# Expert layers by pairs: two experts of 64 token slots each on the two column halves of the matmul array, in float32 on unsplit weights

## The reference

```
lg = xt @ w_rg + b_rg                      # 4 groups; grp = argmax
le = (xt @ w_re + b_re) of that group      # 8 experts in a group; top 2 of softmax
gate = top_p / sum(top_p) * p_grp
for each expert e of 32:
    y_e = (silu(x_e @ w_eg[e]) * (x_e @ w_eu[e])) @ w_ed[e]     # 1024 -> 512 -> 1024
out[token] = sum over its two experts of gate * y_e[token]
```

## Time and profile before

| | us |
|---|---|
| median of three runs | 2326.18 |
| span of the profiled execution, first to last instruction | 2329.0 |
| PE busy in it | 2235.9 |
| `mix_out`, `route`, experts (from the timeline) | 382.9 to 428.1, to 454.4, to 999.3 |

### The profile page before, as it was taken

One profiled execution on the slowest core, in us unless ns is written; L12 is line 12 of the kernel. 1 busy time (PEld: TensorE's weight loads), 2 busy tenths in 40 slices (PEclk: granted clock), 3 DMA queues, 4 the chain that ended last, 5 costly groups with the idle time before them and its releaser, 6 DMA issues. The chain is left out here.

```text
span 2329.0 us, 30346 instructions
## 1 busy us (share of the span) xinstructions
PE 2235.9 (96%) x11961; PEld 1898.9 (82%) x11961; DVE 1801.5 (77%) x2133; ACT 1161.0 (50%) x1215; POOL 138.8 (6%) x237
## 2 busy tenths in 40 slices
PE   7999989999999999999999999999998999999997
PEld 7888768788888888888788887888987888887886
DVE  6887687688989889866888777887796887776545
ACT  4443244577677776744444364333653333464332
POOL 2000100000000000000111001110001111000000
PEclk9999998999999999999999999999999999999999
DMA  8854553499999999954799536994633998445652
GB/s 300 272 138 148 177 172 100 154 375 375 368 372 375 363 376 363 364 165 154 228 373 350 165 114 210 375 349 169 208 127 112 333 357 289 141 129 166 196 181 72
DMA packets 346769, 567.83 MB, mean 244 GB/s; under 512 B 69248, under 2 KB 182400, under 8 KB 346624
## 3 DMA queue, kind: packets, MB, share of 16 engines
q1 hardware_dynamic: 325632, 490.31, 62.0%
q0 software_dynamic: 20992, 75.54, 8.7%
HBM read 564.71 MB, written 1.05 MB: 243 GB/s over the span
## 5 line engine op out<-in xcount | busy, mean ns | idle before, releaser
L321 PE MATMUL ps<-st_hi,sb_h_hi 128*128 128x512 f32 (+1 forms) x728 | 272.1, 374 | 11.7 <-DVE sb_h_lo L1187 4.6
L323 PE MATMUL ps<-st_hi,sb_h_lo 128*128 128x512 f32 (+1 forms) x728 | 265.0, 364 | 0.0
L322 PE MATMUL ps<-st_lo,sb_h_hi 128*128 128x512 f32 (+1 forms) x728 | 264.8, 364 | 0.0
L293 DVE TENSOR_TENSOR es_lo<-es_raw,es_hi 128x2048 fp32r<-128x2048 f32 x87 | 196.9, 2284 | 19.3 <-ACT es_hi L283 18.9
L321 PE MATMUL ps<-ring_hi,sb_h_hi 128*128 128x512 f32 (+1 forms) x504 | 191.2, 379 | 4.2 <-DVE sb_h_lo L832 2.1
L323 PE MATMUL ps<-ring_hi,sb_h_lo 128*128 128x512 f32 (+1 forms) x504 | 188.5, 374 | 0.0
L322 PE MATMUL ps<-ring_lo,sb_h_hi 128*128 128x512 f32 (+1 forms) x504 | 188.2, 373 | 0.0
L293 DVE TENSOR_TENSOR ring_lo<-ring_raw,ring_hi 128x2048 fp32r<-128x2048 f32 (+4 forms) x86 | 155.2, 1806 | 39.8 <-ACT ring_hi L283 39.7
L293 DVE TENSOR_TENSOR st_lo<-ring_raw,st_hi 128x2048 fp32r<-128x2048 f32 (+1 forms) x66 | 148.9, 2255 | 42.8 <-ACT st_hi L283 42.8
L283 ACT CAST es_hi<-es_raw 128x2048 fp32r<-128x2048 f32 x87 | 164.6, 1914 | 23.9 <-DMA es_raw<-in_w_expert_up_dram 17.9
L293 DVE TENSOR_TENSOR st_lo<-st_raw,st_hi 128x2048 fp32r<-128x2048 f32 x64 | 146.3, 2288 | 30.9 <-ACT st_hi L283 30.8
(11 more groups left out here) (798 smaller groups left out, 5383.6 us busy)
## 6 DMA issues: line engine op xcount, KB each, us to landing
t_aw<-in_ada_w_dram POOLq DMA_DIRECT2D x144, 512.0 KB, 6.6
st_raw<-in_ffn_w_in_dram SPq DMA_DIRECT2D x90, 512.0 KB, 5.8
ring_raw<-in_ffn_w_in_dram SPq DMA_DIRECT2D x86, 512.0 KB, 6.0
es_raw<-in_w_expert_gate_dram SPq DMA_DIRECT2D x40, 1024.0 KB, 8.2
es_raw<-in_w_expert_down_dram SPq DMA_DIRECT2D x39, 1024.0 KB, 7.4
es_raw<-in_w_expert_up_dram SPq DMA_DIRECT2D x37, 1024.0 KB, 7.4
ring_raw<-in_w_expert_up_dram SPq DMA_DIRECT2D x27, 1024.0 KB, 7.2
ring_raw<-in_w_expert_down_dram SPq DMA_DIRECT2D x25, 1024.0 KB, 7.2
```

Source lines behind the costliest of these rows:

```text
L293: dve.tensor_tensor(p.at(self.lo[m % self.held]), p.at(self.raw[n % self.slots]), p.at(self.hi[m % self.held]).bitcast(F32), ALU.subtract) ...
L321: pe.matmul(out, a_hi, b_hi, start=start, stop=False, skip_group_check=True)
L322: pe.matmul(out, a_hi, b_lo, start=False, stop=False, skip_group_check=True)
L323: return pe.matmul(out, a_lo, b_hi, start=False, stop=stop, skip_group_check=True)
```

## The change

Experts are taken by pairs, 16 of them. Each expert has 64 slots of its own (before: 128 slots for a group of eight experts). The slots of the two experts of a pair are the two halves of the array's columns: one matmul has 64 stationary columns and writes partitions 0 to 63, the next writes 64 to 127, and each streams the weights of its own expert. They are float32 matmuls on the raw pieces, with no split on ACT and DVE and no `hi` and `lo` (all pieces are `plain`). The ring has 15 raw slots. The result of a pair is split (`y_hi`, `y_lo`) and scattered to all tokens after each pair; slots of two pairs (four experts, a unit) are gathered from the tokens two pairs ahead (`draw`), between the matmuls of the running pair. Weights lie in slots with the row index split as `(p k)`, so that a partition takes 8 KB in one stretch (before 2 KB or 4 KB stretches). `route` ranks tokens by expert instead of by group, on 64 and 80 columns. The pass for overflow now counts experts with over 64 tokens. The first three pieces go out at the start of `mix_out`, ahead of its last four, and `route` sends the next twelve. The core of the diff:

```diff
 def expert_plan(A):
-    deep = lambda w: w.rearrange("(k p) n -> p k n", p=P)
-    for e in range(NG * NE + 1):
-        if e < NG * NE:
-            pieces += [Piece(deep(w[e, a * P:(a + 4) * P, :]), 4, BANK) for w in (wg, wu) for a in (0, 4)]
-        if e:
-            pieces += [Piece(deep(wd[e - 1, u * HB:(u + 1) * HB, :]), 2, 1024) for u in range(2)]
+    deep = lambda w: w.rearrange("(p k) n -> p k n", p=P)
+    for p in range(NP + 1):
+        if p < NP:
+            pieces += [Piece(deep(w[e])[:, a:a + 4, :], 4, BANK, True)
+                       for w in (wg, wu) for a in (0, 4) for e in (2 * p, 2 * p + 1)]
+        if p:
+            pieces += [Piece(deep(wd[e])[:, f:f + 2, :], 2, 1024, True) for f in (0, 2) for e in (2 * p - 2, 2 * p - 1)]
...
+def gather(pe, M, out, perm, c):
+    for i in (2 * c, 2 * c + 1):
+        for w in range(2):
+            for t in range(2):
+                last = pe.matmul(out[:, i % 2 * 256:(i % 2 + 1) * 256], (M.h_hi, M.h_lo)[w][:, t, i:1024:8],
+                                 perm[:, t].rearrange("p x s -> p (x s)"), start=w == t == 0, stop=w == t == 1,
+                                 skip_group_check=True)
...
 (route, SP)
-            S.send(sp, S.slots + 1)
+            S.send(sp, lent + 2)
...
 (experts, PE)
-            def half(e, bank, a):
-                w = S.take(pe)
+            def half(p, bank, a):
+                w = [S.take(pe), S.take(pe)]
                 for kt in range(a, a + 4):
-                    last = product(pe, ps[:, bank, :], M.hg_hi[:, e // NE, kt, :], M.hg_lo[:, e // NE, kt, :],
-                                   w[0][:, kt - a, :], w[1][:, kt - a, :], kt == 0, kt == 7)
-                last.then_inc(S.used, 1)
+                    for h in range(2):
+                        at = (p % 2 * 2 + h) * SL
+                        last = pe.matmul(ps[h * SL:(h + 1) * SL, bank, :], M.hg[p // 2 % 2][:, kt, at:at + SL],
+                                         w[h][:, kt - a, :], start=kt == 0, stop=kt == 7, skip_group_check=True)
+                        if kt == a + 3:
+                            last.then_inc(S.used, 1)
...
+            def down(p, u):
+                w = [S.take(pe), S.take(pe)]
...
+                for f in (2 * u, 2 * u + 1):
+                    for c in range(2):
+                        for h in range(2):
+                            part = slice(h * SL, (h + 1) * SL)
+                            last = pe.matmul(ps[part, sum_bank(p) + c, :], hidT[:, f, part],
+                                             w[h][:, f - 2 * u, c * BANK:(c + 1) * BANK], start=f == 0, stop=f == NF - 1,
+                                             skip_group_check=True)
...
+            for p in range(NP):
+                v = unit_of(p)
+                if p:
+                    pe.wait_ge(silued, p)
+                half(p, 0, 0)
+                if p:
+                    turn(p - 1)
+                if v:
+                    draw(v, 3 * (p % 2))
+                half(p, 0, 4)
+                if p >= 2:
+                    scatter(p - 2, 0)
...
+                half(p, 1, 0)
+                if v:
+                    draw(v, 3 * (p % 2) + 1)
+                if p >= 2:
+                    scatter(p - 2, 1)
+                half(p, 1, 4)
+                if p:
+                    down(p - 1, 0)
+                if v:
+                    draw(v, 3 * (p % 2) + 2)
+                if p:
+                    down(p - 1, 1)
...
 (mix_out, SP)
+            k.experts.send(sp, 3)
             S.send(sp, len(S.pieces))
...
-        k.stream = Stream(nc, "es", expert_plan(A), UNIT, k.shared, (None, None, 0, 1, None), (0, None, None, None)).place(own)
+            k.experts = Stream(nc, "es", expert_plan(A), UNIT, k.shared, (None,) * 13 + (0, 1), ()).place(k.far, "right", 3)
```

More of the change, by code:

```diff
@@ L1382 @@
 HB = 256
+NP, SL = NG * NE // 2, 64
 def expert_plan(A):
@@ L1420, in route @@
[L1420 to L1423, removed]
+        wr, br = k.wr, k.br
+        lt, rest, hit, one, two = (sb(n, [P, NT * R, NE]) for n in ("lt", "rest", "hit", "one", "two"))
+        asg, both = sb("asg", [P, NT, NG, NE]), sb("both", [P, NT, NG, NE])
+        m1, m2, b1 = (sb(n, [P, NT * R]) for n in ("m1", "m2", "b1"))
+        desc, ss, zg = sb("desc", [P, NE]), sb("ss", [P, NT]), sb("zg", [P, NT])
@@ L1488, in _ @@
             pe.wait_ge(q["placed"], 1)
[L1489 to L1509, removed]
+            for c in range(4):
+                gather(pe, M, ps[:, c, :], M.perm[0], c).then_inc(q["gathered"], 1)
+            turn_places(k, pe, ps[:, 4, :], M.perm[0]).then_inc(q["gathered"], 1)
             pe.wait_ge(q["weighted"], 1)
[L1511 to L1514, removed]
+            slot_gates(pe, M, ps[:, 5, :], M.perm[0], 0).then_inc(q["gathered"], 1)
         @block.scalar
@@ L1612, in _ @@
[L1612 to L1622 removed]
+            after(dve.tensor_tensor(both[:], one_e, wide(w1[:]), ALU.mult))
@@ L1847, in program @@
-            copy(n * U + 1, 1)
-        guarded(act, found, program)
-    def vector_pass(dve, found):
-        def take(kind, b, u):
-            dve.wait_ge(high[kind], b + 1)
-            dve.tensor_tensor(lo[kind], raw[u][kind], hi[kind].bitcast(F32), ALU.subtract
-                              ).then_inc(split[kind], 1)
-        def expert(i, n, m, j, final=False):
-            for u in range(U):
-                b = n * U + u
-                more = not (final and u == 1)
-                if more:
-                    take(G, b + 1, 1 - u)
@@ L1862, in expert @@
                 dve.wait_ge(filled[UP], b + 1)
                 dve.wait_ge(silued, b + 1)
[L1865 to L1876 removed]
+                at = M.late_gate[:, m, i:i + 1] if isinstance(i, int) else M.late_gate[:, m, bass.ds(i, 1)]
@@ L1945, in _ @@
             for n in range(2):
-                sp.wait_ge(S.split, S.order[len(S.pieces) - 5 + n] + 1)
+                slot = S.slots - 2 + n
+                final = max(m for m in range(len(S.pieces)) if m % S.slots == slot)
+                sp.wait_ge(S.used, final + 1)
                 N2.send(sp, n + 1)
@@ L2015, in _ @@
+            turn(NP - 1)
+            for c in range(2):
+                last = pe.matmul(ps[:, c, :], k.ones[:], k.gates[:, 1, c * BANK:(c + 1) * BANK], start=True, stop=True)
+            last.then_inc(row_summed, 1)
+            found = first_of(pe)
+            scatter(NP - 2, 0)
+            down(NP - 1, 0)
+            scatter(NP - 2, 1)
+            down(NP - 1, 1)
             late_tensor(pe, found)
-            pe.wait_ge(added, 4 * (NG - 1))
+            pe.wait_ge(added, 4 * (NP - 1))
```

725 lines of the change are left out of this document (325 added, 400 removed).

## The result

The changed kernel takes 2239.23 us (median of four runs, 2238.60 to 2240.18) against 2326.26 us, a ratio of 0.9623 (95% interval 0.9609 to 0.9637). The gain is 87 us. The prediction was 60 us, with 31 to 88 as the likeliest case's own range: sign and mechanism are right, the size is at the far end of that range, one microsecond inside it (the range on record went from 2232 to 2345 us). The profiled execution took 2239.4 us and has a span of 2237.6 us; the span is the shorter one by 1.8 us, as in the other runs of both kernels. So the profiled execution of the kernel before, with its span of 2329.0, was some 4.6 us slower than its median and not 2.8, and gains read from the two traces come out a few us above the 87 us of the medians.

What follows compares the result with a forecast made beforehand. In the experts PE and the transfers both looked full; after the change transfers alone would bound. Earlier start, faster pieces and a shorter end move the experts' end from 999.3 to 939: 2326.2 - 60 = 2266 us, range 2232 to 2345.

Steps and rivals of the forecast that it cites:

- likeliest case: The forecast itself: transfers bound the experts and column halves overlap, gain 60 us, between 31 and 88; chance 0.73.
- The transfers set the end after the change: In the experts, transfers need 32.0 us per pair against PE's 27; last piece lands at 936, PE ends at 939.
- Start and end, 31 us: Expert pieces run without a gap from 431.3, and less PE work follows the last landing: 31 us together.
- The rate: Expert pieces in 8 KB stretches take 2.67 us each instead of 2.82, bounds 2.52 and 2.82.
- The halves run side by side: Expert matmuls on the two column halves overlap: 48 per pair take 20.6 us, at most 25.1, instead of 41.2.
- Rivals 1 and 2: In the experts, column halves run one after another, 2541 us, chance 0.14; or overlap by half, 2376 us, chance 0.06.
- rival 1: Expert column halves run one after another, 47.5 us per pair on PE: 2541 us, chance 0.14.
- PE's pair: PE's whole work for one pair of experts: 27 us, at most 31.4.
- the slack: PE needs less time per expert pair than the transfers, so it idles about 5 us per pair waiting for pieces.
- Rivals 3 and 4: Expert transfers: wide stretches come slower, 2351 us, chance 0.05; or rate stays 372 GB/s, 2295 us, inside the forecast's 0.73.

Runs made afterwards that it cites:

- e5: The changed kernel without the three expert pieces sent during `mix_out`; `route` sends them at its start: 2246.3 us, ratio 0.9649 to the kernel before.
- e6: The changed kernel with normed rows stored so that the gather's weights are read in one stretch, not every eighth element: 2237.7 us.
- e4: The changed kernel with half of every expert piece left out of the transfer, PE doing the same number of matmuls: 2226.8 us.
- e1: The changed kernel with the old row order, so stretches of 2 and 4 KB instead of 8 KB, still 15 slots: 2270.8 us.
- e11: The kernel before with two of the three products per expert matmul, transfers, slots and splits as they were: 2294.6 us.
- e3: The changed kernel with all matmuls of one column half before the other's within each group of 16 rows, not in turns: 2342.4 us.

## Why the prediction was right, and where it was off

**The transfers set the end after the change: right.** e5, e6 and e4 show it together. Start and end, 31 us, were right to a microsecond (30). Of these, 5.1 us of work after the last landing stand where 3.4 were priced, because PE is then still at the group before, and four rows of the scatter follow (905.25 to 906.39).

**The rate: the term that was mis-sized.** "Bounds for a piece: 2.52 us (416 GB/s throughout) and 2.82 us (372 as now). I take the middle, 2.67 us." Measured: 2.49 us, 421 GB/s. Two mistakes made it. The upper bound, 372 GB/s, was taken as a property of the transfers ("the share of 1.02 says that a queue stood behind each transfer all the same"); it was PE's pace, and 394 GB/s is what these stretches give when pieces are issued early enough (e1, e11). So "taking work from PE alone is worth little" was wrong as well: e11 does just that and is 33 us faster. And the lower bound stopped at the best stretch of 4 KB, where the step from 2 to 4 KB, 388 to 416 GB/s in the earlier trace rows, said that 8 KB would lie beyond it. With both, the last landing is 431.3 + 189 x 2.49 = 902; measured 904.9, eight pieces being late by 0.3 to 0.9 us. The range held, but narrowly: the last landing and the end of the experts lie outside their own bounds (904.9 against 908, 910.0 against 911).

The Trainium skill, "HBM Reference", Specifications (TRN2), gives about 425 GB/s for a core that streams alone. The 421 GB/s measured here agree within 1%.

**The halves run side by side: right.** 3.65 us for sixteen rows; "3.4 us" was expected, and the entry makes the rest. One argument for it was slightly off: by its own rows two float32 streams read 512 columns in 0.215 us, 5% faster than one float32r stream (0.227), not "no faster". Rivals 1 and 2 fall. e3 shows what the overlap hangs on, the order of the rows, which the prediction did not price as a condition; even with the wrong order the time is 2342 us and not the 2541 of rival 1.

**PE's pair: 27 us predicted, 28.5 measured, and the slack misread.** The gather was priced from rows with contiguous weights; here every eighth element is a weight, and the weight loads of the changed kernel show it (from 440 to 910 us, mean ns behind the busy time):

```profile
L1410 PEld LDWEIGHTS ps<-ring_lo,moe_h_hi 128*128 128x128 f32 x128 | 36.4, 332 | 12.2 <-issue 12.2
...
L1900 PEld LDWEIGHTS ps<-ring_hi 128*128 128x128 f32 x60 | 11.5, 191 | 15.4 <-issue 14.1
```

The load takes 0.33 us where the scatter's takes 0.19, and a row 0.24; in one stretch (e6) the same load takes 0.20 and a row 0.12. It cost nothing, because 28.5 is still under the transfers' 30. But the 5 us per pair that PE was to idle did not come: it idles for 1.9 us of 350, because it begins eleven pieces behind.

**Rivals 3 and 4** fall with the rate: 8 KB stretches of every other region are not slower. Of the four `w_out` pieces behind the three expert pieces the first lands 7.9 us after its issue (3.6 before), a delay of 4.3 us where the prediction allowed 8.5; the last lands at 404.7 (404.6 before), and `mix_out` and `route` end at 451.4, 3 us earlier than before.

## What to carry to other kernels

A DMA share of 1.0 with a steady rate does not mean that the transfers are the bound; look at how long before the preceding landing each piece was issued, and at what frees its slot. When two engines look full at once, take work from one in an experiment before pricing the other as a limit. Where two sizes of a thing show a trend, draw the bound for a third from the line and not from the better of the two.

## What the runs showed of the hardware

- Three transfers of 1 MiB under way run at 419 GB/s, two at 317, and with two the DMA share still reads 0.89.
- Packets of 2, 4 and 8 KB took 88, 164 and 312 ns (medians; the first two from e1, the third from the changed kernel), and a piece in such stretches 2.71, 2.56 and 2.49 us.
- Float32 matmuls of 64 stationary columns on the two column halves run at the full rate of each, 0.43 us per row and half, when they come in turns. When eight rows of one half come first, the other half starts beside the fifth (515.378 and 515.372 us in e3).
- A weight load of 128 columns whose elements lie 32 B apart takes 0.33 us (0.20 side by side, e6), and matmuls of 256 columns with such loads start every 0.24 us instead of 0.12.
